# Exchanging the halves of the query heads by DMA in place of a rotation matmul

## What is computed

```python
def apply_rope(x, cos, sin):
    x1, x2 = jnp.split(xf, 2, axis=-1)
    return jnp.concatenate([x1 * c - x2 * s, x2 * c + x1 * s], axis=-1)

def swa_mixer(qkv, q_norm, k_norm, sinks, cos, sin):
    q, k, v = split_cols(qkv, SWA_SIZES)
    q = apply_rope(rmsnorm(q.reshape(bsz, s, SWA_HEADS, SWA_HD), q_norm), cos, sin)
    k = apply_rope(rmsnorm(k.reshape(bsz, s, SWA_KV_HEADS, SWA_HD), k_norm), cos, sin)
    ...
    sc = jnp.einsum('bnqkgd,bnjkd->bnkgqj', qb, kb).astype(jnp.float32) * (SWA_HD ** -0.5)
    ...
    m = jnp.maximum(jnp.max(sc, axis=-1, keepdims=True), sink)
    p = jnp.exp(sc - m)
    denom = jnp.sum(p, axis=-1, keepdims=True) + jnp.exp(sink - m)
    o = jnp.einsum('bnkgqj,bnjkd->bnqkgd', p / denom, vb.astype(jnp.float32))
```

## Time and profile before

| | before |
|---|---|
| median of 3 runs | 2749.2 us |
| lowest and highest run | 2742.68 and 2750.34 us |
| profiled execution | 2747.97 us, of which its span 2746.2 |
| TensorE busy in the span | 2634.7 us, 96% |
| DVE, ACT, POOL busy | 64%, 41%, 0% |
| mean granted TensorE clock | 0.985 of full |

### The profile page before, as it was taken

The page is one execution under the profiler, slowest core; times in us unless marked ns, Lnnn a source line. Parts: engine busy times, 40 slices in busy tenths (PEclk is TensorE's granted clock), DMA queues, the critical chain, the costliest instruction groups (busy, mean ns, idle before and its releaser), DMA issues.

```text
span 2746.2 us, 46683 instructions
## 1 busy us (share of the span) xinstructions
PE 2634.7 (96%) x18488; PEld 2442.7 (89%) x18488; DVE 1763.8 (64%) x2497; ACT 1133.2 (41%) x1470; POOL 10.1 (0%) x18
## 2 busy tenths in 40 slices
PE   6898998999999999999999999999899999999999
PEld 5798898899898899889988998899788998899889
DVE  4666667665777764776477666665677647764774
ACT  2334444343444443444344344543344434443443
POOL 0000000000000000000000000000000000000000
PEclk8999999999999999999999999999899999999999
DMA  5343433355445556555555553345255665665554
GB/s 153 100 118 106 116 109 110 120 158 173 146 148 187 186 184 184 184 186 187 182 186 184 158 161 100 93 135 165 85 184 183 191 183 178 185 192 183 181 188 151
DMA packets 429635, 432.64 MB, mean 158 GB/s; under 512 B 15487, under 2 KB 427796, under 8 KB 429108
## 3 DMA queue, kind: packets, MB, share of 16 engines
q1 hardware_dynamic: 422832, 422.63, 50.0%
q0 software_dynamic: 1584, 5.40, 0.7%
q10 hardware_dynamic: 5076, 2.56, 0.3%
HBM read 428.44 MB, written 2.10 MB: 157 GB/s over the span
## 4 chain that ended last, share of the span: by engine, by line
PE 83%; DVE 9%; ACT 4%; issue 2%; DMA 1%; SPq 0%; POOL 0%; ACTq 0%; DVEq 0%
PE stream L1528 24%; PE stream L1513 13%; PE stream L1514 12%; PE stream L1515 12%; PE stream L1529 12%; DVE w_lo L900 2%; PE bank L1607 1%; PE bank L1548 1%; ACT w_hi L492 1%; ACT scores L837 1%; PE bank L1497 1%; PE stream L1607 1%; DMA cst<-in_consts 1%; DMA stage<-in_mem 1%; DVE k_buf L954 0%
## 5 line engine op out<-in xcount | busy, mean ns | idle before, releaser
L900 DVE TENSOR_TENSOR w_lo<-w_raw,w_hi 128x1024 fp32r<-128x1024 f32 x800 | 965.5, 1223 | 605.3 <-ACT w_hi L492 601.5
L492 ACT CAST w_hi<-w_raw 128x1024 fp32r<-128x1024 f32 x800 | 834.8, 1048 | 835.3 <-PE stream L1515 481.1
L1528 PE MATMUL stream<-h,w_hi 128*128 128x512 f32 x2816 | 995.6, 399 | 0.0
L1529 PE MATMUL stream<-h,w_lo 128*128 128x256 f32 x2816 | 790.9, 281 | 0.0
L1528 PEld LDWEIGHTS stream<-h,w_hi 128*128 128x128 f32 x2816 | 529.1, 188 | 131.9
L1513 PE MATMUL stream<-act,w_hi 128*128 128x256 f32 x2016 | 578.5, 287 | 1.0 <-DVE act L927 1.0
L1515 PE MATMUL stream<-act,w_lo 128*128 128x256 f32 x2016 | 571.5, 283 | 0.0
L1514 PE MATMUL stream<-act,w_hi 128*128 128x256 f32 x2016 | 571.4, 283 | 0.0
L1529 PEld LDWEIGHTS stream<-h,w_lo 128*128 128x128 f32 x2816 | 532.0, 189 | 0.1
L1513 PE MATMUL stream<-h,w_hi 128*128 128x256 f32 x1536 | 460.3, 300 | 2.9 <-DVE w_lo L900 2.9
L1514 PE MATMUL stream<-h,w_hi 128*128 128x256 f32 x1536 | 439.6, 286 | 0.0
(11 more groups left out here) (353 smaller groups left out, 1739.5 us busy)
## 6 DMA issues: line engine op xcount, KB each, us to landing
w_raw<-in_ffn_in_w SPq DMA_DIRECT2D x352, 512.0 KB, 4.5
w_raw<-in_ffn_out_w SPq DMA_DIRECT2D x176, 512.0 KB, 4.4
w_raw<-in_hyb_in_w SPq DMA_DIRECT2D x96, 512.0 KB, 3.8
w_raw<-in_swa_in_w SPq DMA_DIRECT2D x48, 512.0 KB, 3.6
w_raw<-in_xkv_w SPq DMA_DIRECT2D x32, 512.0 KB, 3.5
w_raw<-in_hyb_out_w SPq DMA_DIRECT2D x32, 512.0 KB, 3.5
w_raw<-in_swa_out_w SPq DMA_DIRECT2D x32, 512.0 KB, 3.5
w_raw<-in_xq_w SPq DMA_DIRECT2D x16, 512.0 KB, 3.5
```

What stands on the lines that cost most here:

```text
L492: nc.scalar.copy(whi[:, k], raw[:, n % NRAW]).then_inc(hi_split, 1)
L900: v.tensor_tensor(wlo[:, k], raw[:, n % NRAW], whi[:, k].bitcast(F32), ALU.subtract).then_inc(lo_split, 1)
L1528: mm(bank[:, m, :], whi[:, k, kk, w], h[:, kt, :, :], start=(q == 0 and kk == 0), stop=False, skip_group_check=True)
L1529: last = mm(bank[:, m, 0:TOK], wlo[:, k, kk, w], h[:, kt, 0, :], start=False, stop=(q == 3 and kk == len(kts) - 1), skip_group_check=True)
```

## The change

The rotation by matmul of the queries goes. In its place the POOL queue copies `nraw` into `nr` within SBUF, in four DMAs per group, each of 32 partitions by 512 columns (64 KB), so that the two halves of each head change places. The sign of the rotation and the partner's gain move into a sine table with gain and scale (`q_sin`): its gain column is the product of the rotation matrix and the gain vector, a matmul of one column in tick 12, copied out by DVE in tick 13. DVE waits for all four DMAs ahead of the sine product, which it now makes in place in `nr`. The keys' rotation stays a matmul.

```diff
-            q_cos, q_rotm = ang[:, 0, :], ang[:, 1, 0:P]
+            q_cos, q_sin, rot_gain = ang[:, 0, :], ang[:, 1, :], qcol[:, 90:91]
...
             pool.dma_start(sinks[:], a["swa_sinks"].rearrange("a h -> (a h)").partition_broadcast(P)).then_inc(pos_loaded, 16)
+            for g in range(8):
+                pool.wait_ge(group_evac, GROUP[SWQ] + g + 1)
+                pool.wait_ge(q_tables, 1)
+                if g:
+                    pool.wait_ge(q_rot, g)
+                for k in range(4):
+                    to, fr = 32 * k, 32 * (k ^ 1)
+                    pool.dma_start(nr[to:to + 32, :], nraw[fr:fr + 32, :]).then_inc(q_turned, 16)
...
                     ni = N_ROPE + 2 + g
-                    dve.wait_ge(rot_done, g + 3)
                     if g:
                         dve.wait_ge(s_done, g)
-                    v.tensor_tensor(two(nr[:]), two(B[1][:]), sinb[:].unsqueeze(1).to_broadcast([P, 2, TOK]), ALU.mult)
+                    dve.wait_ge(q_turned, 64 * (g + 1))
+                    v.tensor_tensor(two(nr[:]), two(nr[:]), q_sin.unsqueeze(1).to_broadcast([P, 2, TOK]), ALU.mult)
...
-                    v.tensor_scalar(q_rotm, c_("rot"), gain, SWA_HD ** -0.5, ALU.mult, ALU.mult)
+                    dve.wait_ge(rot_gains, 1)
+                    link(v.tensor_copy(rot_gain, B[1][:, 0:1]))
+                    v.tensor_scalar(q_sin, sinb[:], rot_gain, SWA_HD ** -0.5, ALU.mult, ALU.mult)
...
                     ni = N_ROPE + 2 + g
-                    pe.wait_ge(group_evac, GROUP[SWQ] + g + 1)
-                    if g:
-                        pe.wait_ge(q_rot, g)
-                    else:
-                        pe.wait_ge(q_tables, 1)
+                    if g == 0:
                         pe.wait_ge(sv_ready, 2)
-                    mm(B[1][:], q_rotm, nraw[:], start=True, stop=True).then_inc(rot_done, 1)
                     pe.wait_ge(n_sq, ni + 1)
...
+                if t == 12:
+                    mm(B[1][:, 0:1], c_("rot"), pcol("swa_q_norm", 0), start=True, stop=True).then_inc(rot_gains, 1)
```

More of the change, by code:

```diff
@@ L344, in trunk @@
         rot_done, kT_done, ksw_done, ksw_ready = sem("rot_done"), sem("kT_ready"), sem("k_swap_done"), sem("k_swap_ready")
+        q_turned, rot_gains = sem("q_halves_swapped"), sem("rotated_gain")
         q_rot, sv_raw, svT, sv_ready = sem("q_rotated"), sem("swa_v_raw"), sem("swa_v_transposed"), sem("swa_v_ready")
```

## The result

| | before | after |
|---|---|---|
| median of 9 runs each | 2746.89 us | 2755.73 us |
| lowest and highest run | 2741.46, 2750.34 us | 2749.78, 2761.01 us |
| span of the profiled execution | 2746.2 us | 2755.8 us |
| mean granted clock in it | 0.985 | 0.979 |

The ratio after to before is 1.0034 [1.0024, 1.0044]: 8.8 us slower. The time is inside the range. Counted against these nine runs of before, the case that came is "slower by over 0.3%", not the one I held likeliest. The 2755.73 itself lies under the forecast's limit of 2757.4, because that limit was counted from 2749.2 for before, 2.3 us above the median of the nine.

The account below looks back on a forecast made before the run. It took ACT and DVE to set the loop from the third turn on. Terms +0.4 - 0.7 + 0 + 0.2 + 3.2 = +3.1 us on 2747.97 gave 2751.1, forecast as 2752, range 2746 to 2761.

Parts of the forecast that it names:

- slower by over 0.3%: Whole kernel: measured time above the limit of 2757.4 us, chance 0.23; the likeliest case was "same", 0.70.
- What bounds the kernel now: Head-group turns: from the third on, ACT and DVE set the 20.97 us loop; TensorE has 1.4 us to spare.
- Part 1: Removing the 1.13 us rotation matmul from TensorE: worth 0 in turns 2 to 7, -0.7 us in turn 1.
- Part 2: POOL's copies in turns 2 to 7: DVE waits 1.0 us, TensorE's need for q_rot still met, price 0.
- Turn 0: First head-group turn: the late copies eat the gain from the removed matmul, +0.4 us (bounds -0.4 and +2.6).
- Part 3: Building the sine table: one more one-column matmul on TensorE, 0.2 us once (bounds 0 and 0.4).
- Part 4: TensorE's clock in quieter pauses: three of six turns fall instead of one, +3.2 us (bounds 0 and 8.0).
- Every turn loses its clock: TensorE's clock: five falls more than now, +8.0 us, 2757, or 2760 with dearer falls; chance 0.14.
- The transfer lands late: Copies: a piece needing 1.25 us more makes DVE's wait outgrow its cover by 1.0 per turn, 2760; chance 0.13.
- DVE holds POOL up: POOL's last copy issue must wait for DVE's probability scaling: 6 x 0.9 = +5.4 us, 2758; chance 0.07.
- TensorE's time counts everywhere: All turns: the removed matmul's full 8 x 1.13 = 9.0 us comes off, 2740; chance 0.06.
- Nothing moves: Whole kernel: copies' landing hidden and clock as before, 2749; chance 0.09.

Follow-up runs that it names:

- E10: The changed kernel once more, unaltered, one execution for a second profile; 2751.67 us.
- E1: The changed kernel plus one 128x512 matmul with unread result where the rotation matmul stood; 2745.64 us, ratio 1.0004 to the kernel before.
- E7: The changed kernel without copies or DVE's wait, halves not exchanged, plus an unread 128x512 matmul in the rotation's place; 2743.32 us, ratio 0.9992.
- E9: The changed kernel with four unread 64 KB copies per group ahead of the real ones and unread matmuls in both TensorE pauses; 2759.59 us, ratio 1.0056.
- E5: The changed kernel with unread matmuls in both TensorE pauses, one 128x512 and two 128x256; 2744.3 us, ratio 0.9991.
- E2: The changed kernel without the 32 copies and DVE's wait, halves not exchanged, so the matmul's removal alone; 2756.32 us, ratio 1.0038.
- E8: The kernel before with unread 128x256 matmuls: two in the second pause, one ahead of the evacuation wait (four in turn 1); 2736.83 us, ratio 0.997.
- E3: The kernel before, matmul kept, plus four 64 KB copies per group on POOL that nobody reads; 2747.83 us, ratio 1.0011.
- E6: The kernel before, matmul kept, plus two unread 128x256 matmuls in the second pause, ahead of the transposes; 2743.07 us, ratio 0.9991.

## Why the prediction was right in kind and short in size

**What bounds the kernel now: right.** An undisturbed turn is 20.96 with or without 1.13 us of TensorE work, and the transposes start behind L1405 as forecast. The waits ahead of the head sums and of the transposes came out at 1.12 and 1.15 us, forecast 1.1 and 1.3. The chain of turn 2 after, as in the earlier trace rows, has the same links:

```profile
1687.14 0.68 DVE norm_raw L918
...
1689.46 1.23 DVE scores L1405
1690.74 1.09 PE bank L1508 x8
...
1695.14 0.68 PE bank L1964 x6
...
1699.60 1.47 ACT scores L846 x7
...
1704.81 2.36 DVE w_lo L909 x2
1708.10 0.68 DVE norm_raw L918
```

**Part 1: right.** Worth 0 in turn 2; turn 1 went from 23.08 to 22.39, -0.69 where I took -0.7. That compares two turns with the same fall, at a clock of 0.85. That the profiled execution after fell in the same way there is luck: in E10 turn 1 had the smaller fall and lasted 21.89. My 0 for the exchange in turn 1 also held only beside the fall; at the full clock it was 0.81 (E1 against E7).

**Part 2: right, by errors that nearly cancel.** POOL's issues, their landing and who waited:

```profile
L478 POOL DMA_DIRECT2D norm_r<-norm_raw x32: 496/498/519, 1644.7 to 1801.6; - x32
...
  DVE norm_r L1427: 9.4, 8
...
DMA to landing us min/median/max: 2.1/2.8/3.9
```

In turn 2 the evacuation ended at 1687.82 and POOL began at 1688.11, 0.29 later, which I had left out. The issues took 0.50 each, not 0.56, and the last copy landed about 2.9 us after its issue began, not 3.2. DVE's timeline there:

```profile
1692.49 0.69 DVE L1427 TENSOR_TENSOR norm_r<-norm_r,angle 128x512 f32<-128x512 f32 x1 [0.67 <-DMA norm_r<-norm_raw]
...
1693.81 0.69 DVE L1429 TENSOR_TENSOR q_rot<-norm_raw,norm_r 128x512 f32<-128x512 f32 x1
```

The sine product came at E + 4.67 (forecast 4.9), DVE waited 0.67 us (1.0), and L1429 ended at 1694.50 with 0.48 us left (0.25) before TensorE's L1964:

```profile
1694.98 0.84 PE L1964 MATMUL bank<-ba_hi,ba_lo 128*128 128x128 f32 x6
```

E9 shows that this cover is thin and real: about 1 us later is 0.7 us a turn. E1's turn 6 and E5's turn 4 show its end: there a wait of DVE of 1.15 and 1.18 us cost 0.2. The Trainium skill's estimate (DMA: Bandwidth & Descriptors, Anatomy of one DMA) of 2.15 us for 64 KB is met by the fastest copy, 2.1; the median was 2.8 and the slowest 3.9, so the neighbouring row's 3.2 was nearer to the median than the estimate was.

**Turn 0: right in sign, +0.72 for +0.4.** The chain of turn 0 after runs over the transfer:

```profile
1643.70 0.70 DVE norm_raw L918
...
1644.68 1.49 POOL norm_r L478 x3
1646.17 3.24 DMA norm_r<-norm_raw
1649.43 0.69 DVE norm_r L1427
...
1650.76 0.70 DVE q_rot L1429
1651.51 0.95 PE bank L1964 x6
```

From E = 1644.40 to the end of L1429, at 1651.46, are 7.06 us; I had 6.9. E10 had +0.81.

**Part 3: right.** The one-column matmul stands between two evacuations of the key and value projection. The start of the one ahead of it (L909 before, L918 after) and of the one behind it:

```profile
1617.65 0.69 DVE L909 TENSOR_TENSOR norm_raw<-stream,rstd 128x512 f32<-128x512 f32 x1
1628.48 0.69 DVE L909 TENSOR_TENSOR norm_raw<-stream,rstd 128x512 f32<-128x512 f32 x1 [0.62 <-PE stream L1515]
```
```profile
1620.70 0.69 DVE L918 TENSOR_TENSOR norm_raw<-stream,rstd 128x512 f32<-128x512 f32 x1
1631.75 0.69 DVE L918 TENSOR_TENSOR norm_raw<-stream,rstd 128x512 f32<-128x512 f32 x1 [0.62 <-PE stream L1526]
```

That is 10.83 us before and 11.05 after, +0.22 where I took 0.2; E10 has 11.05 too.

**Part 4: this term was mis-sized.** The step was "three of the six turns fall, where one does now, +2 x 1.59 = +3.2 (bounds 0 and 8.0)". Five of the six turns 2 to 7 fell, and so did the gap behind turn 7. Its wait was the one that I had counted as not followed by a fall. Some falls cost 2.78 (23.75 - 20.97), above the 2.11 that I held the dearest. Measured by the turns it is 5.55 + 0.74 = +6.3 in the profiled execution after; the second profile gave 6.7 for turns 2 to 6 alone. The sum with 6.3 in it comes to -0.69 + 0.72 + 0.22 + 6.3 = +6.55, and the ratio says 6.6 to 12.1, so between nothing and 5.5 us may lie outside these terms. I had the mechanism and its bounds, and placed the size by halves, from one wait that was followed by a fall and one that wasn't. The rows before could have warned me: one of six turns already fell with the matmul in place. The Trainium skill (TensorE: Matmul & The Clock Gate, Part 1) says that the throttled clock is the default and that activity releases it. The runs agree as to the direction: E2 fell in every turn from 1 on, and with the quiet filled (E5, E8) none fell behind turn 1. That this favours a fall in every turn was my reading of it, and turn 2 kept its clock in both profiles of the changed kernel.

**The rivals.** *Every turn loses its clock* is the nearest to what came, but for turn 2, which both profiles of this kernel had whole. I gave it 0.14. Its 2757 is 1.3 us from the median. *The transfer lands late* and *DVE holds POOL up* did not come: 32 issues within 496 to 519 ns, and E2 loses as much without copies. What the landing did cost lay almost wholly in the first two turns: +0.72 in turn 0, and 0.81 in a turn 1 at the full clock. *TensorE's time counts everywhere* is excluded by turn 2's length. *Nothing moves* fell by the clock.

**Open.** Why turn 2 keeps its clock in both profiles when turns 3 to 6, equal in instructions and pauses, lose theirs; why the falls of the kernel before lie in turns 1 and 5 in one execution and in turns 2 and 6 in E3's; the last 0.1% of E3; the part of the 8.8 us between the medians beyond the 6.55 that the profile shows; and the part of E9's 14 us beyond the 9.1 that its turns 0 to 6 show.

## What to carry to other kernels

Work on an engine that is not the limit can still be worth its time: in a stretch of short waits and tiny matmuls, take the engine's clock as a term of its own, count how many like stretches already fall, and expect more to fall when dense work goes. Where TensorE must wait anyway, a matmul whose result nobody reads was free here, and in both pauses such matmuls made the kernel before 0.3% faster. Where TensorE is itself late they cost time (1.02 us in E6's turn 1). Test such a suspicion of the clock with a dummy in the removed work's place before looking at the new transfers.

## What the runs showed of the hardware

- The clock fell behind two waits of about 1.1 us with eight tiny matmuls between them, without any long wait, in each of the turns 3 to 7 and in neither turn 2 of the changed kernel's two profiles. A turn with a fall is 1.3 to 1.6 us or 2.6 to 2.8 us longer (22.30 to 22.58, and 23.61 to 23.75); no turn 2 to 6 with a fall lies in between.
- The clock fell although TensorE counts as busy in the tiny passes of the head sums for 1.05 us between the waits. With a matmul of 128x512 ahead of them two of turns 2 to 6 fell (E1), with two more of 128x256 behind them none (E5).
- Copies within SBUF of 32 partitions by 2 KB on the POOL queue: 0.50 us to issue, 2.1 to 3.9 us to land, 0.29 us from the end of DVE's instruction to POOL's first. With four more ahead of them, the real ones landed in 2.2 to 2.3 us (median), and in E9's turn 2 the exchange was 1.0 us later instead of the 2.0 that four issues take.
